# Splitting s4 at the end of a tile's turn, the first tile's weights in product order, and four feed-forward tiles split inside the loop

## The reference, cut to what matters

```
def swiglu_ffn(h, w_gate_up, w_down):
    gate, up = jnp.split(h @ w_gate_up, 2, axis=-1)
    return (jax.nn.silu(gate) * up) @ w_down
...
h = rms_norm(x, p['norm_ffn'][layer])
x = x + swiglu_ffn(h, p['ffn_w_gate_up'][layer], p['ffn_w_down'][layer])
```

## Time and profile before

| what | value |
|---|---|
| median of 3 runs | 2155.36 us (2155.02 to 2155.96) |
| the profiled execution: its own time | 2151.29 us |
| the profiled execution: its span | 2149.4 us |
| busy share of the span: TensorE, VectorE, ScalarE, GpSimd | 92%, 61%, 35%, 10% |
| mean granted TensorE clock | 0.982 of full speed |
| TensorE idle ahead of seven-product matmuls | 75.8 us |

### The profile page before, as it was taken

One profiled execution on the slowest core, in us unless ns is written; L12 is line 12 of the kernel. 1 busy time (PEld: TensorE's weight loads), 2 busy tenths in 40 slices (PEclk: granted clock), 3 DMA queues, 4 the chain that ended last, 5 costly groups with the idle time before them and its releaser, 6 DMA issues. The chain is left out here.

```text
span 2149.4 us, 46995 instructions
## 1 busy us (share of the span) xinstructions
PE 1967.5 (92%) x20156; PEld 1839.4 (86%) x20156; DVE 1303.8 (61%) x2008; ACT 748.2 (35%) x1460; POOL 205.8 (10%) x291
## 2 busy tenths in 40 slices
PE   8998999999988888998999888879998988888998
PEld 8997779997988888997988867669996988888897
DVE  5346877445788878435557643447554677877632
ACT  2005874013344445001237434343213244444311
POOL 5000001000100000010000344410100200000000
PEclk9999999999999999999999999999999999999999
DMA  4234213460323233232222000033350222322232
GB/s 132 79 122 139 60 32 95 125 192 20 89 79 86 82 89 89 81 90 59 61 78 60 7 4 5 4 83 109 98 167 21 81 84 83 89 80 85 68 87 77
DMA packets 299406, 170.37 MB, mean 79 GB/s; under 512 B 10328, under 2 KB 294176, under 8 KB 299200
## 3 DMA queue, kind: packets, MB, share of 16 engines
q1 hardware_dynamic: 294976, 151.25, 24.7%
q10 hardware_dynamic: 4224, 16.12, 1.9%
HBM read 155.94 MB, written 11.41 MB: 78 GB/s over the span
## 5 line engine op out<-in xcount | busy, mean ns | idle before, releaser
L260 PE MATMUL psum<-words_r,weights_high_r 128*128 128x272 f32 (+1 forms) x5248 | 899.5, 292 | 17.5 <-DVE words_r L211 6.4
L260 PEld LDWEIGHTS psum<-words_r,weights_high_r 128*128 128x128 f32 x5248 | 757.6, 190 | 30.4 <-issue 26.3
L260 PE MATMUL psum<-words_r,weight_ring_r 128*128 128x272 f32 (+1 forms) x2624 | 565.9, 289 | 0.0
L260 PEld LDWEIGHTS psum<-words_r,weight_ring_r 128*128 128x128 f32 x2624 | 422.3, 191 | 0.0
L211 DVE TENSOR_TENSOR weight_ring_r<-weight_ring,weights_high_r 128x512 fp32r<-128x512 f32 (+2 forms) x344 | 330.7, 961 | 7.3 <-ACT weights_high_r L351 1.2
L2126 PE MATMUL psum<-words_r,weights_high_r 128*128 128x272 f32 x1280 | 251.2, 293 | 75.8 <-ACT words L2136 68.1
L206 DVE TENSOR_SCALAR weights_high_r<-weight_ring 128x1024 fp32r<-128x1024 f32 (+1 forms) x178 | 122.3, 687 | 308.6 <-PE psum L260 304.4
L2126 PEld LDWEIGHTS psum<-words_r,weights_high_r 128*128 128x128 f32 x1280 | 204.0, 191 | 84.0 <-issue 75.9
L2126 PE MATMUL psum<-words_r,weight_ring_r 128*128 128x272 f32 x640 | 187.8, 293 | 0.0
L2126 PE MATMUL psum<-words_r,sum_high 128*128 128x272 f32 x960 | 185.8, 290 | 0.0
L2126 PEld LDWEIGHTS psum<-words_r,sum_high 128*128 128x128 f32 x960 | 152.9, 191 | 0.0
(11 more groups left out here) (372 smaller groups left out, 2474.2 us busy)
## 6 DMA issues: line engine op xcount, KB each, us to landing
weight_ring<-in_ffn_w_gate_up_dram SPq DMA_DIRECT2D x88, 512.0 KB, 3.8
weight_ring<-in_xa_w_kv_dram SPq DMA_DIRECT2D x32, 512.0 KB, 4.0
weight_ring<-in_ffn_w_down_dram SPq DMA_DIRECT2D x32, 448.0 KB, 3.6
weight_ring<-in_sb_w_qkv_dram SPq DMA_DIRECT2D x24, 512.0 KB, 3.8
weight_ring<-in_xa_w_q_dram SPq DMA_DIRECT2D x16, 512.0 KB, 3.7
weight_ring<-in_xa_w_o_dram SPq DMA_DIRECT2D x16, 512.0 KB, 3.8
weight_ring<-in_ffn_w_down_dram SPq DMA_DIRECT2D x16, 512.0 KB, 3.7
weight_ring<-in_sb_w_o_dram SPq DMA_DIRECT2D x8, 512.0 KB, 3.7
```

What stands on the lines that cost most here:

```text
L260: last = nc.tensor.matmul(c.psum[0:job.m(u), job.bank(q) + h, 0:w], weights[:, k, :], x[:, k, h * w:(h + 1) * w], start=job.opens(u) and k ...
```

## The change

Four things move; nothing is computed that was not computed before, and no matmul, split or load is added or removed.

1. In the loop, the high part of s4(n) goes on ScalarE from ahead of snapshot 2 to the end of tile n's turn, and its low part on VectorE to the end of the turn as well. The low part of a22(n) goes up to second place of the turn. The two buffers of s4 lie in another region.
2. Ahead of the loop, VectorE makes the first tile's sums and low parts in the order of the products (a11, s1, s2, a12, s3), with the low parts of t2, t3, t4 between them, where before the low part of t2, the sum s4, the low part of t3 and `gate(1)` stood ahead of a11.
3. In the loop, hidden tiles 0 to 3 are split at the ends of turns 6, 9, 12 and 15. The region of the t factors is moved by 4 x 544 + 64 words so that the four high parts have room.
4. After the loop the remaining splits are put in another order, and the scaling and multiplying of tile 20 go behind ten of them.

```
-        q, w = 4 * HALF, 4 * P
+        q, w, at = 4 * HALF, 4 * P, 4 * T + 64
...
-        self.sum_at = {"s1": [8 * q] * 2, "s2": [8 * q + w] * 2, "s4": [8 * q + 2 * w, 8 * q + 3 * w]}
+        self.sum_at = {"s1": [(5, at + 8 * q)] * 2, "s2": [(5, at + 8 * q + w)] * 2, "s4": [(9, 3 * T), (9, 5 * T)]}
...
+    early = [6, 9, 12, 15]
...
     def hidden_high(act, n):
         act.wait_ge(multiplied, n + 1)
-        act.wait_ge(*seven.done(("s1", "s2", "s3", "a22", "s4", "s4")[n // 4], last_tile))
+        if n >= 4:
+            act.wait_ge(*seven.done(("s1", "s2", "s3", "a22", "a22")[n // 4 - 1], last_tile))
...
                 seven.snapshot(act, 1, n)
-                seven.take_high(act, "s4", n)
                 if n < last_tile:
                     seven.take_high(act, "a11", n + 1)
                 else:
-                    for j in range(4):
+                    for j in range(4, 7):
                         hidden_high(act, j)
                 seven.snapshot(act, 2, n)
                 if n < last_tile:
                     for s in ("s1", "s2", "a12", "s3"):
                         seven.take_high(act, s, n + 1)
-            for j in range(4, 8):
+                if n in early:
+                    hidden_high(act, early.index(n))
+                seven.take_high(act, "s4", n)
+            for j in range(7, 10):
                 hidden_high(act, j)
             silu(act, FT - 2)
-            for j in range(8, 16):
+            for j in range(10, 16):
...
             seven.take_t_low(dve, "t1")
-            seven.take_t_low(dve, "t2")
-            for s in ("s1", "s3", "s2", "s4"):
+            for s in ("s1", "s3", "s2"):
                 seven.sum(dve, s, first)
-            seven.take_t_low(dve, "t3")
-            gate(1)
             seven.take_low(dve, "a11", first)
             seven.take_low(dve, "s1", first)
+            seven.take_t_low(dve, "t2")
+            seven.sum(dve, "s4", first)
             seven.take_low(dve, "s2", first)
+            gate(1)
             seven.take_low(dve, "a12", first)
+            seven.take_t_low(dve, "t3")
+            seven.take_low(dve, "s3", first)
+            scale_up(1)
             seven.take_t_low(dve, "t4")
-            scale_up(1)
-            seven.take_low(dve, "s3", first)
+            seven.take_low(dve, "a22", first)
             multiply(dve, 1)
             for n in range(first, last_tile):
                 seven.sum(dve, "s1", n + 1)
+                if n > first:
+                    seven.take_low(dve, "a22", n)
                 seven.sum(dve, "s3", n + 1)
                 seven.sum(dve, "s2", n + 1)
-                seven.take_low(dve, "a22", n)
                 seven.gate_half(dve, "c11", n)
-                seven.take_low(dve, "s4", n)
                 seven.take_low(dve, "a11", n + 1)
...
                 seven.take_low(dve, "s3", n + 1)
+                seven.take_low(dve, "s4", n)
                 if n > first:
                     multiply(dve, n - 1)
+                if n in early:
+                    hidden_low(dve, early.index(n))
             seven.take_low(dve, "a22", last_tile)
+            hidden_low(dve, 4)
             seven.gate_half(dve, "c11", last_tile)
-            seven.take_low(dve, "s4", last_tile)
-            for j in range(4):
-                hidden_low(dve, j)
+            hidden_low(dve, 5)
+            hidden_low(dve, 6)
             seven.up_second(dve, last_tile)
             split_unit(c, dve, down, 0, 0)
             seven.gate_half(dve, "c12", last_tile - 1)
+            seven.take_low(dve, "s4", last_tile)
             seven.scale_gate(dve, last_tile - 1)
-            for j in range(4, 8):
-                hidden_low(dve, j)
+            hidden_low(dve, 7)
             seven.up_first(dve, last_tile)
-            seven.scale_up_second(dve, last_tile)
-            multiply(dve, last_tile - 1)
+            hidden_low(dve, 8)
+            hidden_low(dve, 9)
             split_unit(c, dve, down, 0, 1)
             seven.gate_half(dve, "c12", last_tile)
             seven.scale_gate(dve, last_tile)
-            for j in range(8, 16):
+            for j in range(10, 15):
                 hidden_low(dve, j)
+            seven.scale_up_second(dve, last_tile)
+            multiply(dve, last_tile - 1)
+            hidden_low(dve, 15)
             multiply(dve, last_tile)
```

More of the change, by code:

```diff
@@ L1962, in __init__ @@
         self.c, self.x, self.gain, self.up, self.hidden, self.gated, self.norm = c, x, gain, up, hidden, gated, norm
-        q, w = 4 * HALF, 4 * P
+        q, w, at = 4 * HALF, 4 * P, 4 * T + 64
         self.t_full, self.x_parts = {}, {}
         for i, t in enumerate(("t1", "t2", "t3", "t4")):
-            self.t_full[t] = c.region(5, 4, HALF, (2 * i + 1) * q)
-            self.x_parts[t] = (c.region(5, 4, HALF, 2 * i * q, F32R), c.region(5, 4, HALF, (2 * i + 1) * q, F32R))
+            self.t_full[t] = c.region(5, 4, HALF, at + (2 * i + 1) * q)
+            self.x_parts[t] = (c.region(5, 4, HALF, at + 2 * i * q, F32R), c.region(5, 4, HALF, at + (2 * i + 1) * q, F32R))
         for b, k, h in (("b11", 0, 0), ("b21", 4, 0), ("b22", 4, 1)):
@@ L2002, in words @@
             return ring[:, (2 * n + i) % RING, k:k + 4, :]
-        return self.c.flat(5, 4 * P, self.sum_at[s][n % 2], dtype).rearrange("p (k n) -> p k n", k=4)
+        region, at = self.sum_at[s][n % 2]
+        return self.c.flat(region, 4 * P, at, dtype).rearrange("p (k n) -> p k n", k=4)
     def bank(self, s, n):
@@ L2366, in _ @@
             seven.x_less(dve, "t3", 1, seven.b12, seven.b12_ready)
-            dve.wait_ge(seven.t_ready["t2"], 4)
             seven.x_less(dve, "t4", 0, seven.t_full["t2"], seven.t_ready["t2"])
             seven.take_t_low(dve, "t1")
-            seven.take_t_low(dve, "t2")
-            for s in ("s1", "s3", "s2", "s4"):
+            for s in ("s1", "s3", "s2"):
                 seven.sum(dve, s, first)
-            seven.take_t_low(dve, "t3")
-            gate(1)
             seven.take_low(dve, "a11", first)
             seven.take_low(dve, "s1", first)
+            seven.take_t_low(dve, "t2")
+            seven.sum(dve, "s4", first)
             seven.take_low(dve, "s2", first)
+            gate(1)
             seven.take_low(dve, "a12", first)
+            seven.take_t_low(dve, "t3")
+            seven.take_low(dve, "s3", first)
+            scale_up(1)
             seven.take_t_low(dve, "t4")
-            scale_up(1)
-            seven.take_low(dve, "s3", first)
+            seven.take_low(dve, "a22", first)
             multiply(dve, 1)
```

## The result

The changed kernel takes 2078.16 us (median of 4 runs) against 2155.66 us before (4 runs beside it): ratio 0.9638 [0.9618, 0.9658], 77.5 us faster. In a second set it took 2072.82 against 2153.92 us, 0.9626 [0.9605, 0.9647], 81.1 us. The forecast was 2074.6, or 80.8 us less. The profiled execution took 2078.25 us.

The account below looks back on a forecast made before the run. TensorE bounds the kernel, stalling once per tile for ScalarE's snapshot. Loop 68.4 + first tile 2.6 + end 9.8 = 80.8 us off 2155.36 gives 2074.6 us, range 2066 to 2089.

Parts of the forecast that it names:

- The loop, 68.4 us: Tile loop: TensorE's stall goes whole in tiles 3 to 20, 18 tiles x 2 layers x 1.90 us.
- a rival with 0.10: Loop: VectorE becomes the bound, a tile takes 11.0 us, gain 65.3 us, 2090 us; chance 0.10.
- The rival of slower loads: Loop: up-unit loads slow each other; landing at 9.5 us makes the kernel 13 us slower, 2168 us; chance 0.03.
- The first tile, 2.6 us: Ahead of the loop: s2 starts 3.0 us early less 1.7 for a clock fall, 1.3 us per layer.
- one fall of the clock per layer: First tile: the clock falls behind the new 2.1 us gap at s2, costing 1.7 us in each layer.
- all 3.0: First tile: s2 starts at 598.55 instead of 601.54, 3.0 us early; 6.0 for both layers if the clock holds.
- from there to the next tile nothing changes: First tile: after s2, the course up to the next tile stays as before, so s2's lead is kept.
- The end, 9.8 us: After the loop: unit 2 of the down projection starts earlier, by 5.0 us in layer 0 and 4.8 in layer 1.
- the scale of the prediction: Last tile's timetable: zero is the start of a11 of the last tile, 832.9 before in layer 0, 1976.5 in layer 1.
- eight low parts took 6.86 us instead of 5.2: End, layer 0: this slower stretch was carried over, moving unit 2's effective start from 29.9 to 31.6.
- the four falls: Clock falls counted behind first-tile and unit 2 gaps; without them the sum is 87.6, 2067.8 us; clock-holds rival's chance 0.10.
- as long as the 2.07 us gap: First tile: a gap as long as the 2.07 us one behind which the clock fell counts 1.7 us for a fall.

Follow-up runs that it names:

- e1: Kernel before with only the order inside the tile loop changed (s4's halves, a22's low part); 2087.06 us, ratio to before 0.9688.
- e5: Changed kernel with two spare VectorE operations (128x544, result unused) behind s4's low part in each turn; 2086.96 us, 0.9699.
- e7: Changed kernel with 8 unused matmuls ahead of s2 of the first tile and 8 ahead of down unit 2; 2068.94 us, 0.9607.
- e8: Changed kernel with GpSimd's two low-rank scalings (layer 0 only) held back until down unit 2 is done; 2072.19 us, 0.9608.
- e6: Changed kernel with snapshot 0 of the first tile ahead of silu of tile 1 on ScalarE; 2077.11 us, 0.9622.
- e3: Changed kernel with only VectorE's low part of s4 back in its old place; 2154.26 us, ratio to before 0.9998.
- e11: Combined kernel (e9's waits, e8's line, e7's first filling) with the last tile's s4 low part ahead of unit 0's split and c12; 2066.18 us, 0.9592.
- e9: Changed kernel where down units 0 to 2 wait for split hidden tiles one by one; 2069.42 us, 0.9602.
- after_again: The changed kernel run once more, nothing altered, beside the later kernels; 2072.82 us, 0.9626.
- e4: Changed kernel with one spare VectorE operation (128x544, result unused) behind s4's low part in each turn; 2072.64 us, 0.9628.

## Why the prediction was right, and where its terms were off

- **The loop, 68.4 us.** Measured 18 turns x 2 x (12.47 - 10.57), as s4's first matmuls stand: 34.3 us in each layer, 68.6. e1 gives 68.7 by itself. That VectorE doesn't become the bound, a rival with 0.10, came out by a room of 0.9 us (0.85 forecast); e5 shows the point where it does. The rival of slower loads is out too: the gate-up loads land after 3.7/3.8/4.7 us (shortest, median, longest), before 3.6/3.8/4.7.
- **The first tile, 2.6 us.** From t1's low part to s4(2) it now takes 25.5 us in layer 0 and 24.4 in layer 1 against 26.8 and 26.7: 1.2 + 2.3 = 3.6. The step that was off is one fall of the clock per layer. One of two came. A fall costs 1.52 us from s2 to a22 (1.7 forecast). A held clock doesn't give back all 3.0: s2 starts 9.54 us behind t1's low part, not 9.36, and "from there to the next tile nothing changes" didn't hold in layer 1, where a11 of tile 3 loses 0.36 us to its late low part.
- **The end, 9.8 us.** Measured 4.2 + 6.3 = 10.5, from s4(20) to the stage's end. On the scale of the prediction (s4(20) being 7.6) s4(21) starts at 11.6, unit 1 at 20.6, and unit 2 at 30.0 in layer 0 and 28.3 in layer 1; forecast 11.5, 20.4, 29.9 without the fall, and 28.2. These starts were right; what was off is the clock behind them: in layer 1 it held, and in layer 0 it was at 0.50 for 5.0 us, 2.5 us lost where 1.7 stood in the sum (e7, which filled that gap, gains the same 2.5). So 5.0 became 4.2 and 4.8 became 6.3, errors of opposite sign, and that the sum of this term is near is in part luck. Luck too is one step inside it. I carried over to layer 0 that eight low parts took 6.86 us instead of 5.2, and had no cause for it. The cause is in the trace of before: GpSimd's scalings run there beside two of the eight, and the same eight of layer 1 take 5.17.

```profile
857.83 2.68 POOL L1924 TENSOR_TENSOR words<-words,vector_columns 128x512 f32<-128x512 f32 x2 [286.20 <-DMA words<-in_rw_g_dram]
...
1999.74 5.17 DVE L211 TENSOR_TENSOR words_r<-words,words_r 128x544 fp32r<-128x544 f32 x8
```

After, the low parts ahead of unit 2 take their 0.65 us each; the scalings meet the half gate and the scaling ahead of them and cost 1.7 us there, as e8 shows. The size carried over because the collision came back at another place.

- **The sum.** 68.6 + 3.6 + 10.5 = 82.7 in the stages. The loop, five sixths of it, came out as derived; the 1.9 us above the forecast are mostly the two falls of the clock that didn't come, less what one of the others cost more. The medians' differences, 77.5 and 81.1, lie below it; the profiled run's deficit is traced to the unchanged code above, that of the medians I don't know run by run.
- **The rule on gaps.** The Trainium skill (TensorE: Matmul & The Clock Gate, section "Why this matters for your kernels") warns of idle gaps from a length that lies between the 2.24 and 3.93 us measured here. By it three of the four falls would not come and that behind 3.93 us would. I let all four fail to come, since I had overlooked that my own figures put unit 2 of layer 0 at 28.2 + 1.7 = 29.9, which is 4.2 us behind unit 1's end and not 2.4. The trace agrees with the page at 3.93, 2.24 and 2.12 us and not at 2.14. Over all runs neither it nor my rule "as long as the 2.07 us gap" holds: gaps of 2.1 us ended in a fall in 8 of 16 layers, and e1 held behind 3.60. Half a fall for each such gap is what the sum should have held.
- **The noise.** I took the 0.04% between three runs for the kernel's spread. Before ran from 2147.24 to 2161.38 us in one later set and from 2148.19 to 2165.72 in another. The effect is 3.6%, so no verdict hangs on it, but e6 to e8 can't be told from after by their times.

## What to carry to other kernels

When a stall names an engine, look at what stands in its queue ahead of the late work and for whom that waits; move it to where its condition is met anyway, and move its consumer on every other queue too (e3, e11). Let a consumer wait for the piece that it needs next and not for the whole (e9: 8.5 us in the stages, 3.4 in the medians, for one moved wait). Read small effects from the length of the stage that was changed, since unchanged stages may differ by 10 us between two traces.

## What the runs showed of the hardware

- Behind equal gaps of 2.12 to 2.15 us the granted clock fell in 8 layers and held in 8. It also fell after 1.82 us (0.67 in e6, 3.6 us behind another wait of 0.66), and held after 1.67, 1.46 and 1.49 us. Of longer gaps, it fell behind all eight of 3.88 to 3.94 us (0.50 to 0.66, in before, after, after_again, e1, e3 and e4) and held behind 3.34 and 3.60 us in e1 (1.00). Matmuls without use in the gap prevented it 6 times of 6.
- GpSimd's 128x512 multiplications beside VectorE's 128x272 and 128x544 operations made these 1.28 and 1.56 us instead of 0.43 and 0.71. The Trainium skill (Trainium Architecture — The Big Picture, section "What this means for kernel authors") says that these two engines contend for a port pair, as an exclusive lock; the trace agrees that they hinder each other, and doesn't show how.
- The recurrence stage, thousands of 64x64 matmuls with idle time between, took 209.4 to 221.5 us for the same code, at a granted clock of 0.99 and 0.94. The clock isn't all of it: after and e8 both had 0.96 and differ by 4.7 us. What makes the rest is open.
